# A two-block network's expert placing: the weight moves from the first key's one-hots to the second key's, and the builders are dealt out anew

## The reference

```python
q = (xb @ w_q).reshape(PEER_TOKEN_BLOCK, PEER_HEADS, 2, PEER_HALF)
s = jnp.einsum('thcd,hcnd->thcn', q, sub_keys)
s_top, i_top = lax.top_k(s, PEER_TOPK)
cand = s_top[:, :, 0, :, None] + s_top[:, :, 1, None, :]
cand_idx = i_top[:, :, 0, :, None] * PEER_KEYS + i_top[:, :, 1, None, :]
best, pos = lax.top_k(cand, PEER_TOPK)
expert = jnp.take_along_axis(cand_idx, pos, axis=-1)
gates = jax.nn.softmax(best, axis=-1)
u_sel, v_sel = u_tab[expert], v_tab[expert]
act = jax.nn.gelu(jnp.einsum('td,thkd->thk', xb, u_sel))
return jnp.einsum('thk,thkd->td', gates * act, v_sel)
```

## Time and profile before

| | us |
|---|---|
| median of three runs (lowest, highest) | 2358.3 (2356.9, 2359.8) |
| span of the profiled execution | 2357.1 |
| placing, first stretch (groups 0 to 26, with `choose`) | 65.6 |
| gap between the stretches | 4.3 |
| placing, second stretch (groups 27 to 63) | 53.8 |
| last stage | 498.9 |
| TensorE, VectorE, GpSimd, ScalarE busy over the span | 2254.7, 1777.9, 745.3, 748.7 |

### The profile page before, as it was taken

How to read it: one execution, slowest core, us unless ns; L and a number is a source line. 1 busy time by engine, 2 the same in 40 slices (tenths; PEclk the granted TensorE clock), 3 DMA queues, 4 the chain that set the end, 5 groups by cost and what they waited for, 6 DMA issues and landing times.

```text
span 2357.1 us, 30495 instructions
## 1 busy us (share of the span) xinstructions
PE 2254.7 (96%) x11914; PEld 1934.6 (82%) x11914; DVE 1777.9 (75%) x3437; ACT 748.7 (32%) x1028; POOL 745.3 (32%) x688
## 2 busy tenths in 40 slices
PE   8999999999999999999999999999778899999991
PEld 7888888889999998989888888888777666766661
DVE  8666777678999897665798897656889865666669
ACT  4345556544344433444111111111566301000000
POOL 0000000000000000000566644566457555666665
PEclk9999999999999999999999999999999999999996
DMA  6544444546854443565898998999820499999998
GB/s 225 184 187 169 162 175 157 197 167 187 244 177 166 162 174 143 183 225 218 307 408 318 413 390 343 414 410 414 316 86 28 166 414 415 413 414 414 413 414 331
DMA packets 128591, 633.09 MB, mean 269 GB/s; under 512 B 14656, under 2 KB 14656, under 8 KB 86080
## 3 DMA queue, kind: packets, MB, share of 16 engines
q1 hardware_dynamic: 48816, 346.64, 38.5%
q0 software_dynamic: 74736, 275.81, 30.6%
q10 hardware_dynamic: 4896, 8.70, 1.2%
HBM read 626.84 MB, written 4.26 MB: 268 GB/s over the span
## 4 chain that ended last, share of the span: by engine, by line
PE 70%; DMA 15%; DVE 9%; POOL 2%; ACT 2%; issue 1%; ACTq 0%; DVEq 0%; POOLq 0%
PE ps L1019 19%; DMA work<-in_peer_v_rows,weight_raw 14%; PE ps L709 14%; PE ps L712 7%; PE ps L663 6%; PE ps L686 5%; PE ps L687 5%; PE ps L693 5%; PE ps L978 4%; DVE scan_ws L2236 3%; DVE work L2221 2%; POOL work L613 2%; DVE ps L2193 1%; PE ps L1056 1%; DMA scan_ws<-second_kept 1%
## 5 line engine op out<-in xcount | busy, mean ns | idle before, releaser
L2236 DVE SCALAR_TENSOR_TENSOR scan_ws<-work,weight_raw,scan_ws 128x1024 f32<-128x1024 f32 x254 | 326.4, 1285 | 156.1 <-DMA work<-in_peer_v_rows,weight_raw 151.2
L1065 PE MATMUL ps<-weight_raw,pairs 128*128 128x512 f32 x1024 | 440.9, 593 | 1.9 <-DMA weight_raw<-in_peer_v_dense 1.2
L1019 PE MATMUL ps<-work,weight_raw 128*128 128x256 f32 x2048 | 442.5, 379 | 0.0
L1019 PEld LDWEIGHTS ps<-work,weight_raw 128*128 128x128 f32 x2048 | 389.1, 190 | 52.6
L1065 PEld LDWEIGHTS ps<-weight_raw,pairs 128*128 128x128 f32 x1024 | 303.7, 297 | 137.2 <-DMA weight_raw<-in_peer_v_dense 1.9
L1680 DVE TENSOR_TENSOR weight_low<-weight_raw,weight_high 128x2048 fp32r<-128x2048 f32 x145 | 332.0, 2290 | 102.0 <-ACT weight_high L1163 101.9
L613 POOL DMA_INDIRECT work<-in_peer_v_rows,weight_raw x256 | 314.4, 1228 | 183.2 <-DVE scan_ws L2236 121.5
L709 PE MATMUL ps<-operand_parts,weight_high 128*128 128x512 f32 x1456 | 354.9, 396 | 3.4 <-DVE slots L1666 1.2
L709 PEld LDWEIGHTS ps<-operand_parts,weight_high 128*128 128x128 f32 x1456 | 268.9, 188 | 61.1 <-issue 7.5
L1163 ACT ACTIVATE weight_high<-weight_raw 128x2048 fp32r<-128x2048 f32 x145 | 276.7, 1908 | 76.8 <-PE ps L712 71.2
L2184 DVE SCALAR_TENSOR_TENSOR work<-work,scan_ws 128x1024 f32<-128x1024 f32 x184 | 222.3, 1225 | 104.5 <-DMA work<-in_peer_u_rows,weight_raw 102.4
(11 more groups left out here) (292 smaller groups left out, 2662.7 us busy)
## 6 DMA issues: line engine op xcount, KB each, us to landing
weight_raw<-in_w_in SPq DMA_DIRECT2D x120, 1024.0 KB, 4.8
weight_raw<-in_peer_u_dense SPq DMA_DIRECT2D x64, 1024.0 KB, 8.1
weight_raw<-in_peer_v_dense SPq DMA_DIRECT2D x64, 1024.0 KB, 8.0
weight_raw<-in_w_out SPq DMA_DIRECT2D x32, 1024.0 KB, 4.8
weight_raw<-in_peer_w_q SPq DMA_DIRECT2D x13, 1024.0 KB, 7.6
weight_raw<-in_conv_w_out SPq DMA_DIRECT2D x8, 1024.0 KB, 4.9
weight_raw<-in_ssm_w_val SPq DMA_DIRECT2D x8, 1024.0 KB, 4.7
weight_raw<-in_ssm_w_gate SPq DMA_DIRECT2D x8, 1024.0 KB, 4.8
```

Of the source, the lines that this page charges most:

```text
L1019: mm = nc.tensor.matmul(ps[:, 6 + s % 2, h * T:(h + 1) * T], w[:, h, k, :], gained_u[:, k, :], start=(k == 0), stop=(k == KU - 1))
L1065: mm = nc.tensor.matmul(ps_v[:, t, c, :], pairs[:, i // QKEYS, t * P:(t + 1) * P, i % QKEYS], w[:, i % 2, c * 512:(c + 1) * 512], start=(i ...
L2236: v.scalar_tensor_tensor(out=y_tok[:, t, :], in0=row_at(s), scalar=pick_w[:, g:g + 1], in1=y_tok[:, t, :], op0=ALU.mult, op1=ALU.add).then ...
```

## The change

GpSimd's groups come in two kinds now. In a P group (0, 1 and 2) all is as before. In a W group GpSimd builds the second key's one-hots with the weight in them, by a TENSOR_SCALAR with two operations and two per-partition operands, and VectorE builds plain first-key one-hots with one TENSOR_TENSOR for four tokens. A V group is VectorE's alone (weighted first key, plain second key), an A group has ScalarE for the second key. The roles of groups 0 to 63 are

```diff
 ALONE = GROUPS_T - 5
-POOLED = list(range(ALONE)) + list(range(ALONE + 1, TT * GROUPS_T, 3))
-ACTED = list(range(ALONE + 2, TT * GROUPS_T, 3))
+PREBUILT = 3
+ROLES = "".join("V" if g % 6 == 2 else "W" for g in range(PREBUILT, ALONE - 1)) + "WVWAV" + "AVWAWVW" * 5
+ROLE = ("P" * PREBUILT + ROLES)[:TT * GROUPS_T]
+POOLED = [g for g in range(TT * GROUPS_T) if ROLE[g] in "PW"]
+ACTED = [g for g in range(TT * GROUPS_T) if ROLE[g] == "A"]
 ROTATED = [g for g in range(TT * GROUPS_T) if g not in ACTED]
 DRAIN_SLABS = 3
+EARLY_AT = POOLED[8]
+VALUE_AT = next(g for g in POOLED if g > ALONE)
...
             for n, g in enumerate(POOLED):
-                if g == 8:
+                if g == EARLY_AT:
                     for early in (2, 3):
                         value_row(early)
-                elif n == ALONE:
+                elif g == VALUE_AT:
                     value_row(4)
...
                         pool.wait_ge(pair_done, ROTATED[ROTATED.index(g) - 3] + 1)
-                    pool.wait_ge(pair_ready, ROTATED[ROTATED.index(g) - 2] + 1)
+                if ROLE[g] == "W":
+                    pool.wait_ge(weights_placed, g // GROUPS_T + 1)
                 for a in range(GROUP):
                     tok = GROUP * g + a
-                    ins = nc.gpsimd.tensor_scalar(hot_at(g)[:, a, :], iota_key, second_t[:, tok:tok + 1], None, ALU.is_equal)
+                    if ROLE[g] == "W":
+                        ins = nc.gpsimd.tensor_scalar(hot_at(g)[:, a, :], iota_key, second_t[:, tok:tok + 1], weight_t[:, tok:tok + 1],
+                                                      ALU.is_equal, ALU.mult)
+                    else:
+                        ins = nc.gpsimd.tensor_scalar(hot_at(g)[:, a, :], iota_key, second_t[:, tok:tok + 1], None, ALU.is_equal)
                 ins.then_inc(second_hot_ready, 1)
...
             def weights_out(t):
 
                 dve.wait_ge(w_turned, t + 1)
-                own.do(v.tensor_copy(weight_t[:, t * P:(t + 1) * P], ps_turn[:, 2 * P + t * P:2 * P + (t + 1) * P]))
+                v.tensor_copy(weight_t[:, t * P:(t + 1) * P], ps_turn[:, 2 * P + t * P:2 * P + (t + 1) * P]).then_inc(weights_placed, 1)
+                dve.wait_ge(weights_placed, t + 1)
+
+            def plain_hot(hot, keys, g):
+
+                return v.tensor_tensor(hot, iota_key.unsqueeze(1).broadcast_to([P, GROUP, P]),
+                                       keys[:, GROUP * g:GROUP * (g + 1)].unsqueeze(2).broadcast_to([P, GROUP, P]), ALU.is_equal)
 
             def place(g):
 
                 if g > 1:
                     dve.wait_ge(pair_done, g - 1)
+                if ROLE[g] == "W":
+                    plain_hot(first_hot[:, g % 2, :, :], first_t, g).then_inc(pair_ready, 1)
+                    return
                 for a in range(GROUP):
                     tok = GROUP * g + a
                     ins = v.tensor_scalar(first_hot[:, g % 2, a, :], iota_key, first_t[:, tok:tok + 1], weight_t[:, tok:tok + 1], ALU.is_equal, ALU.mult)
-                if g in POOLED or g in ACTED:
-                    ins.then_inc(pair_ready, 1)
-                else:
-                    v.tensor_tensor(hot_at(g), iota_key.unsqueeze(1).broadcast_to([P, GROUP, P]),
-                                    second_t[:, GROUP * g:GROUP * (g + 1)].unsqueeze(2).broadcast_to([P, GROUP, P]), ALU.is_equal).then_inc(pair_ready, 1)
+                if ROLE[g] == "V":
+                    plain_hot(hot_at(g), second_t, g).then_inc(pair_ready, 1)
+                else:
+                    ins.then_inc(pair_ready, 1)
```

More of the change, by code:

```diff
@@ L115 @@
 TILES = TILE_WQ + 16
+SLABS = 64 + 16 + 56 + 8 + 16 + 16
 PLAIN = 2
@@ L380, in build @@
         raw_landed = [sem(f"raw_landed{b}") for b in range(NSLAB)]
-        params_in, ssm_in, b_in, c_in, subk_in = (sem(n) for n in ("params_in", "ssm_in", "b_in", "c_in", "subk_in"))
+        params_in, ssm_in, matrices_in = (sem(n) for n in ("params_in", "ssm_in", "matrices_in"))
         gain_turned, gain_spread, gain_ready = sem("gain_turned"), sem("gain_spread"), sem("gain_ready")
@@ L412, in build @@
         x_kept, x_back_in = sem("x_kept"), sem("x_back_in")
-        tail_landed = [sem(f"tail_landed{n}") for n in range(RING)]
         u_done, u_evicted, v_done = sem("u_done"), sem("u_evicted"), sem("v_done")
@@ L421, in build @@
             sem(n) for n in ("whole_turned", "dots_ready", "gelu_ready", "w_ready", "w_turned"))
+        weights_placed = sem("weights_placed")
         pair_ready, pair_done, pair_copied = sem("pair_ready"), sem("pair_done"), sem("pair_copied")
@@ L432, in freed, with tail_count @@
             return n + PSLOTS
+        def tail_count(n):
+            return 16 * (SLABS // NSLAB + n // RING + 1)
         M_B = 0
@@ L473, in _ @@
                 if t == NSLAB:
-                    sp.dma_start(b_nat, d["ssm_b"]).then_inc(b_in, 16)
+                    sp.dma_start(b_nat, d["ssm_b"]).then_inc(matrices_in, 16)
                 load(w_in, 4 * KH + t, TILE_IN + t + 1)
@@ L482, in _ @@
                     sp.wait_ge(y_final, 1 + KH)
-                    sp.dma_start(ct, d["ssm_c"]).then_inc(c_in, 16)
+                    sp.dma_start(ct, d["ssm_c"]).then_inc(matrices_in, 16)
             for t, (kind, n) in enumerate(BRANCH):
@@ L498, in _ @@
             sp.wait_ge(merged, KD)
-            sp.dma_start(subt, d["peer_sub_keys_2"]).then_inc(subk_in, 16)
+            sp.dma_start(subt, d["peer_sub_keys_2"]).then_inc(matrices_in, 16)
             for t in range(4, 16):
@@ L504, in _ @@
                     sp.dma_start(w_q_early[n], w_q[PRELOADED[n]]).then_inc(q_landed[n], 16)
+            assert len(slab_ends) == SLABS and SLABS % NSLAB == 0
             def load_tail(n, src):
-                sp.dma_start(w_raw[:, n % RING, :], src).then_inc(tail_landed[n % RING], 16)
+                sp.dma_start(w_raw[:, n % RING, :], src).then_inc(raw_landed[n % RING], 16)
             for n, t in enumerate(QUERY_RING):
@@ L969, in query_slab @@
                 at = QUERY_RING.index(n)
-                pe.wait_ge(tail_landed[at % RING], 16 * (at // RING + 1))
+                pe.wait_ge(raw_landed[at % RING], tail_count(at))
                 return w_raw[:, at % RING, :].rearrange("p (k n) -> p k n", k=KD)
@@ L1012, in pair_tiles @@
                 n = U_AT + s
-                pe.wait_ge(tail_landed[n % RING], 16 * (n // RING + 1))
+                pe.wait_ge(raw_landed[n % RING], tail_count(n))
                 if s > 1:
@@ L1097, in _ @@
             pe.wait_ge(first_out, 2)
-            pe.wait_ge(subk_in, 16)
+            pe.wait_ge(matrices_in, 48)
             score(ps[:, 5, :], 0, 0).then_inc(first_scored, 1)
@@ L1331, in ssm_matrices @@
                 elif n == 12:
-                    act.wait_ge(c_in, 16)
+                    act.wait_ge(matrices_in, 32)
                     c_im = ct[:, 1].rearrange("p a b -> p (a b)")
@@ L1830, in _ @@
             input_tile(LAM_AFTER + 3)
-            dve.wait_ge(b_in, 16)
+            dve.wait_ge(matrices_in, 16)
             own.do(v.memset(b_diag, 0.0))
```

## The result

The changed kernel takes 2384.47 us (median; 2376.28 to 2398.04) where the kernel before takes 2359.03 (median of four). The ratio on record is 1.0114, 95% interval 1.0082 to 1.0146; that of the two medians is 1.0108. It is 25 us slower; 9.5 us faster was forecast, and the range ended at 2363.

A forecast was written before the change was run, and what follows sets the result against it. VectorE was taken to bound placing, with GpSimd replacing it. Savings of 3.1 us (place 0 to 26) and 6.4 us (place 27 to 63), together 9.5, took 2358.3 to 2348.8 us; range 2337 to 2363.

The forecast's parts named there:

- The bound of before: Placing: VectorE bounds it, a steady first-stretch step takes 2.39 us, and time saved moves the unchanged last stage equally.
- VectorE's new unit costs: VectorE in placing: 0.60 us per four-token compare, 0.28 per single-token build, so 1.67 per W step against 2.39.
- GpSimd becomes the bound: Placing: GpSimd replaces VectorE as limit at 2.67 us per W group, saving 3.1 us to place 26 and 6.4 after.
- e = 0.02: GpSimd's W one-hots: the second operation with its per-partition operand adds 0.02 us each, within 0 to 0.06.
- 0.088: Added us per GpSimd one-hot for the second operation at which the forecast gain of 9.5 us is gone.
- dear second operation: Rival, chance 0.17: GpSimd's second operation costs much more; at 0.15 us per one-hot the kernel takes 2367.0 us.
- The compare at 0.28: Placing: each four-token VectorE compare delays GpSimd by 0.28 us, the middle between 0 and 0.56.
- the absorbed case: Rival, chance 0.20: GpSimd's gaps absorb the compares at no cost and the second operation is free; 2338.5 us.
- the full lock: Rival, chance 0.14: each VectorE compare stops GpSimd for 0.56 us, a W group takes 2.95; 2361.9 us.
- the third rival: Chance 0.17: the second operation is expensive on GpSimd, over 140 one-hots on the path; slower by over 0.2% from 0.12 us.
- The gap: Between the two placing stretches, 1800.10 to 1804.43: unchanged, worth nothing; its growth would show the prediction wrong.
- Edits at nothing: Changed semaphores for matrix loads, tail loads and weight copy cost nothing, at worst a tenth of a microsecond, twice.

The follow-up runs named there:

- second_p: Changed kernel without W groups: roles of the kernel before for groups 0 to 26, then P, A and V with GpSimd taking half; 2353.8 us, ratio 0.9969.
- after_again: The changed kernel run once more, unchanged, to see its spread; 2380.83 us, ratio 1.0086.
- plain_single: Changed kernel with one-operation GpSimd one-hots in W groups (weights left out) and VectorE's four-token compare there replaced by four single-token instructions; 2355.06 us, ratio 0.999.
- after_plain: Changed kernel with the second operation taken out of GpSimd's W one-hots, so their weights are left out of the result; 2355.32 us, ratio 0.9983.
- fewer_w_halves: Changed kernel with fewer W and more V groups, and each four-token VectorE compare cut into two of two tokens; 2366.06 us, ratio 1.0019.
- fewer_w: Changed kernel with V and W alternating in the first stretch and one W of each seven groups made V in the second; 2363.61 us, ratio 1.0014.
- fewer_w_lead: Changed kernel with fewer W and more V groups, and VectorE's share of each choose issued one step later; 2356.97 us, ratio 0.998.

## Why the prediction was wrong

*The bound of before: right.* VectorE was what TensorE waited for, and its busy time fell by 11.5 us in the first stretch. One limit to it: `second_p` has the same VectorE work per step and takes 2.31, so the 2.39 of the steady step wasn't VectorE's fixed price. The last stage kept its length in all fourteen profiles (498.0 to 500.6), so what placing lost arrived in the span whole: placing +20.7 in `after_again`, span +21.4.

*VectorE's new unit costs: right.* The compares keep a median of 0.68 us and their shortest distance of 0.60 us, also beside a full GpSimd. GpSimd is the one that mostly yields; 5 of the 50 compares in `after_again` take 772 to 854 ns, where the longest of the kernel before takes 686.

*GpSimd becomes the bound: right,* and that is why the next term weighed so much.

*e = 0.02: the step that failed.* Measured 0.773 - 0.577 = 0.196, ten times the value taken and three times the upper bound of 0.06. The bound came from VectorE's rows. It was right for VectorE, by `plain_single` for this very tile (0.06), and wrong to carry over to GpSimd. The argument that most of an instruction isn't per operation rested on no row; it even holds (0.577 of the 0.773 is there with one operation), but it bounds nothing. The prediction had named the point from which this decides, 0.088. It gave the dear second operation a chance of 0.17, with the missing GpSimd row as the argument for it and VectorE's 0.06 against. It should have read that absence as width: on 140 one-hots each 0.1 us is 14 us, more than the whole gain. By the prediction's own count the term is 140 x (0.196 - 0.02) = 24.6 us.

*The compare at 0.28: too low.* In the first stretch of `after_again` GpSimd's path is 1813.3 - 1737.7 = 75.6; less 84 x 0.773 and the gathers' 2.3 leaves 8.4 for 24 compares, 0.35 each; `after_plain` in the same way, less a wait of 0.78, gives 0.38. In the second stretch the 14 W groups run 1823.04 to 1877.46, 54.4 less 0.3 of waiting and 56 x 0.773 = 43.3, so 10.8 for 23 compares, 0.47 each. With 0.35 and 0.47, that is 24 x 0.07 + 23 x 0.19 = 6.1 us more than forecast. Neither the absorbed case (0) nor the full lock (0.56) is right on the mean; a compare of 0.60 takes some three to four fifths of its time from GpSimd. These are upper figures: all that exceeds GpSimd's undisturbed price is put down to the compares here, and in `plain_single` groups with no compare beside them exceed their 2.31 by up to 0.19 as well.

With the two terms the sum is -9.5 + 24.6 + 6.1 = +21.2, against +20.7 measured in placing. With e measured instead of guessed, the third rival would have been the forecast: 2348.8 + 24.6 = 2373.4, and 2379.5 with the compares, where `after_again` has 2380.83.

*The gap: right within 1 us* (3.4 for 4.3), and its feared growth didn't come. *Edits at nothing: right,* by `after_plain` and `second_p`, which keep the new semaphores and are not slower. The wait for the second weights is there, 4.3 us of GpSimd's idle time until the copy at 1822.58; W 33 starts 6.3 after place 27 where 5.7 was counted.

*What would show it.* The test named for e was the shortest duration: 590 to 620 ns for, 680 or more against; 780 answered. Place 26 came at 1813.3 and not 1797, the first value matmul at 1879.4 and not 1849. The waits view did not turn to GpSimd's line as foreseen, but to "issue", as shown above.

*The Trainium skill's two rules.* SBUF — State Buffer, section "Who interferes with whom", holds here: the VectorE form with two SBUF inputs costs GpSimd time, the form with one much less (2.80 against 2.43 a group, 2.31 undisturbed). The lock for the whole instruction isn't what the mean shows: 0.35 to 0.47 of the 0.60. The estimate from GPSIMD Engine Reference, section "Performance pitfalls for Q7 kernels", 0.085 us for an operand read that doesn't overlap, lies beside the measured 0.083 of the per-partition operand. That the mechanism is the same isn't shown; and the larger part, 0.115 for the second operation, was in neither.

## What stays open

Of the first four times of the changed kernel two are 2376.3 and 2376.5, and two are 2392 and 2398; the four of `after_again` are all below 2382. The profiled one is of the latter, and its 18 us before place 0 arise in earlier stages, whose computation the change leaves alone (of their semaphores it replaces some, also that of the loads of line 1038's slabs, but `after_again` has the same ones and no such delay). By the waits, 12.0 of them are idle time of TensorE in two spots, 2.7 us around 1185 and 9.3 from 1284 to 1296; the rest isn't accounted for. The busy time from 1260 to 1300 us, first of the changed kernel, then of `after_again`:

```profile
1260.00:1300.00 40.00, 30.68 (x127) 25.29 (x126) 27.93 (x64) 4.34 (x4) 27.63 (x27) 0.85 1.00 395
```

```profile
1260.00:1300.00 40.00, 40.00 (x187) 35.29 (x186) 28.67 (x66) 6.41 (x6) 32.38 (x26) 1.00 0.99 381
```

TensorE stands still between single matmuls, and the row of its timeline names nothing that it waits for:

```profile
1286.36 0.59 PE L1038 MATMUL ps<-work,weight_raw 128*128 128x256 f32 x2 [1.72 <-issue]
1288.48 0.58 PE L1038 MATMUL ps<-work,weight_raw 128*128 128x256 f32 x1 [1.54 <-issue]
```

The granted clock is 0.85 over these 40 us. `fewer_w_halves` shows 9.5 us of the same, from 1285 to 1298. In both cases the DMA engines' share is 1.0, but it is 0.99 in the undisturbed execution too, so that explains nothing by itself. The kernel before has long executions too (in the last group three of 35 are over 2370, for a median of 2362.19), but none of those was profiled. The cause stays open.

## To carry to other kernels

When work moves to an engine that becomes the bound, the price of one instruction there must come from a row of that engine and that form; where there is none, multiply the count on the path by a wide bound before choosing a value, since here 140 instructions turned 0.18 us into 25, more than twice the expected gain. An engine with slack before the change may have none after it, so give it only the cheap form of the work (`second_p`) and leave the weight on the engine that takes it for 0.06 us. Where an engine feeds a consumer and also waits for the consumer's results, reading those one step later can break a circle of waits (`fewer_w` against `fewer_w_lead`, 8 us in the first stretch).

## What the runs showed of the hardware

- GpSimd's one-hot on 128x128 f32: 0.577 us with one operation, 0.691 with a second on a constant, 0.774 with a second on a per-partition operand. VectorE's on the same tile: 0.196 with one operation, 0.260 with two and a per-partition operand (`plain_single`).
- A VectorE compare with two SBUF tensor inputs, 0.60 us, costs a busy GpSimd 0.35 to 0.47 us on the mean, by an estimate that puts all of the disturbance down to it; two half-sized ones cost the same together. Two whole ones beside the same one-hot add up: it takes 1.45 us in `after_plain`, five times, for 0.59. VectorE's compare keeps its median of 0.68; a tenth of them take 0.77 to 0.85 (`after_again`).
- A single execution of this kernel can lose 10 us or more to TensorE stalls before the stage that is changed, so the landmarks of two executions should be compared before a stage is blamed.
